# Two attentions on one core: products split and gating moved in the second, scaling and two peaks moved in the first

## The reference

```python
# first attention: 8 heads, two softmaxes per head, causal, blocks of 128 queries
s = einsum('bhqd,bshd->bhqs', qb, k) * scale
probs = softmax(where(mask, s, -inf))
a = probs(qb1, k1) - lam * probs(qb2, k2)
o = einsum('bhqs,bshe->bhqe', a, v)            # 128 values per head
o = rms(o, subln) * (1 - lambda_init) * silu(g)
x = x + o @ w_out

# second attention: 16 heads, stick breaking, causal, blocks of 128 queries
z = einsum('bhqd,bshd->bhqs', qb, k) * scale
log_1mb = where(mask, log_sigmoid(-z), 0)
suffix = cumsum(log_1mb, reverse) - log_1mb
a = where(mask, exp(log_sigmoid(z) + suffix), 0)
o = einsum('bhqs,bshe->bhqe', a, v)            # 64 values per head
x = x + (o * silu(g)) @ w_out
```

## Time and profile before

| | |
|---|---|
| median of 3 runs | 2500.83 us (2500.43 to 2504.84) |
| profiled execution, its own time | 2500.57 us |
| its span, first to last instruction | 2498.8 us |
| PE busy | 2352.5 us (94%) |
| DVE busy | 1519.7 us (61%) |
| ACT busy | 967.0 us (39%) |
| mean granted TensorE clock | 0.982 of full speed |

### The profile page before, as it was taken

How to read it: one execution, slowest core, us unless ns; L and a number is a source line. 1 busy time by engine, 2 the same in 40 slices (tenths; PEclk the granted TensorE clock), 3 DMA queues, 4 the chain that set the end, 5 groups by cost and what they waited for, 6 DMA issues and landing times.

```text
span 2498.8 us, 30214 instructions
## 1 busy us (share of the span) xinstructions
PE 2352.5 (94%) x12850; PEld 1248.1 (50%) x12850; DVE 1519.7 (61%) x1962; ACT 967.0 (39%) x1383; POOL 213.5 (9%) x258
## 2 busy tenths in 40 slices
PE   6999999999999999999999777899999997888899
PEld 3445444444444444444444455654444445766664
DVE  6898756644554355697631589955544307888861
ACT  5245334221212123333321476732223116777741
POOL 0001030000000002433202001022000000000000
PEclk9999999999999999999999899999999998999999
DMA  4010001211101110111110000110221100000021
GB/s 179 34 68 34 1 34 38 97 55 47 68 34 63 39 68 34 36 61 75 68 68 34 1 1 1 52 51 34 85 118 41 63 1 34 1 1 1 1 85 51
DMA packets 50328, 116.02 MB, mean 46 GB/s; under 512 B 2387, under 2 KB 7820, under 8 KB 49809
## 3 DMA queue, kind: packets, MB, share of 16 engines
q1 hardware_dynamic: 48456, 105.40, 11.9%
q10 hardware_dynamic: 1736, 8.68, 0.8%
HBM read 101.49 MB, written 12.58 MB: 46 GB/s over the span
## 4 chain that ended last, share of the span: by engine, by line
PE 79%; DVE 12%; ACT 6%; issue 2%; DMA 1%; ACTq 0%; POOL 0%; DVEq 0%
PE PS L72 76%; PE PS L75 4%; ACT RG L81 3%; DVE RG L107 2%; DVE R L101 2%; DVE R L93 2%; DVE mx L110 2%; DVE RG L101 1%; ACT OV L84 1%; DVE scl L110 1%; DMA RG<-in_a_w_in 1%; DVE RG L93 1%; ACT R L81 1%; DVE oss L110 1%; DVE mx L96 0%
## 5 line engine op out<-in xcount | busy, mean ns | idle before, releaser
L72 PE MATMUL PS<-R,RG 128*128 128x512 f16 (+1 forms) x5472 | 1167.6, 375 | 12.2 <-DVE RG L101 5.9
L72 PEld LDWEIGHTS PS<-R,RG 128*128 128x128 f16 (+1 forms) x5472 | 544.0, 104 | 632.2 <-issue 13.2
L72 PE MATMUL PS<-RG,R 128*128 128x512 f16 x2880 | 630.6, 379 | 3.5 <-DVE R L101 3.0
L72 PEld LDWEIGHTS PS<-RG,R 128*128 128x128 f16 x2880 | 281.7, 98 | 334.4 <-DVE R L101 3.5
L81 ACT ACTIVATE R<-PS,scl 128x512 f32<-128x512 f32 (+1 forms) x192 | 126.7, 686 | 711.6 <-PE PS L72 595.0
L101 DVE SCALAR_TENSOR_TENSOR R<-PS,scl,R 128x512 f32<-128x512 f32 (+1 forms) x208 | 148.6, 746 | 146.7 <-PE PS L72 121.6
L107 DVE TENSOR_TENSOR_SCAN RG<-RG 128x127 f32<-128x127 f32 (+7 forms) x128 | 168.6, 1345 | 109.9 <-ACT RG L81 109.6
L72 PE MATMUL PS<-R,OV 128*128 128x64 f32 (+2 forms) x1456 | 191.9, 284 | 33.3 <-DVE R L93 31.2
L101 DVE SCALAR_TENSOR_TENSOR RG<-RG,scl 128x4096 f16<-128x4096 f32 (+1 forms) x43 | 188.6, 4387 | 56.4 <-ACT RG L81 56.4
L72 PEld LDWEIGHTS PS<-R,OV 128*128 128x128 f32 x1456 | 179.1, 198 | 43.3 <-DVE R L93 37.7
L75 PE MATMUL PS<-ident,RG 128*128 128x128 f32 x864 | 149.4, 290 | 48.3 <-ACT OV L84 23.9
(11 more groups left out here) (123 smaller groups left out, 1541.0 us busy)
## 6 DMA issues: line engine op xcount, KB each, us to landing
RG<-in_w_ff SPq DMA_DIRECT2D x16, 2048.0 KB, 8.5
RG<-in_a_w_in SPq DMA_DIRECT2D x8, 2048.0 KB, 8.3
RG<-in_w_in SPq DMA_DIRECT2D x4, 2048.0 KB, 9.8
xspill<-R ACTq DMA_DIRECT2D x2, 4096.0 KB, 15.1
RG<-in_w_kv SPq DMA_DIRECT2D x4, 2048.0 KB, 8.0
RG<-in_b_w_in SPq DMA_DIRECT2D x4, 2048.0 KB, 7.9
R<-in_x SPq DMA_DIRECT2D x8, 512.0 KB, 9.2
RG<-in_w_out SPq DMA_DIRECT2D x2, 2048.0 KB, 7.8
```

The source lines that it names most:

```text
L72: return self.engine.matmul(*a, **k) if self.engine else Nothing()
```

## The change

In the second attention, PE's products of group u - 2 are cut into two halves by blocks of 128 keys: the first half stays behind the transposes of part 0, the second half goes behind the transposes of part 1. DVE's gating of group u - 3 moves from behind the scan of group u to ahead of it.

In the first attention, the scaling of the maxima leaves DVE: ACT scales them in place with a Copy activation just ahead of the Exp that uses them, and waits for its own result. It does this once for each group up to row 3, and once for each side from row 4 on. ACT's Square moves ahead of `exp(u, 1)`. The peak of GG's last tile and `o_peak` move from before the loop to the end of turn 3; `measure(31)` becomes four reductions of 1024 columns at the ends of turns 8 to 11 and a small one in turn 12.

```diff
@@ tensor, second attention
-                    if part == 0 and u >= 2:
+                    if u >= 2:
                         v = u - 2
                         i, hs = sb_groups[v]
-                        for x, h in enumerate(hs):
+                        blocks = [(x, h, j) for x, h in enumerate(hs) for j in range(i + 1)]
+                        mid = len(blocks) // 2
+                        for x, h, j in blocks[mid:] if part else blocks[:mid]:
                             g = h // 8
-                            if h % 8 == 0:
+                            if h % 8 == 0 and j == 0:
                                 banks.take_at(("pvb", i, g), 7)
                                 e.wait_ge(*banks.free(("pvb", i, g)))
                                 e.wait_ge(*sig("bank_act").at("v2", 1, NT - 1))
...
-                        mm.then_inc(*full.up("pvb", i, hs[-1]))
+                        if part:
+                            mm.then_inc(*full.up("pvb", i, hs[-1]))
@@ vector, before and in the first attention
+            def gate_peak(t):
+                e.wait_ge(*sig("gg_gain").at(t))
+                e.tensor_reduce(col(32 + t), GG[:, t, :], AX.X, ALU.max, apply_absolute_value=True).then_inc(*step.up())
...
-                e.wait_ge(*sig("gg_gain").at(t))
-                e.tensor_reduce(col(32 + t), GG[:, t, :], AX.X, ALU.max, apply_absolute_value=True).then_inc(*step.up())
-            e.wait_ge(*step.last())
-            e.tensor_reduce(col(123), col(32, 8), AX.X, ALU.max).then_inc(*sig("o_peak").up())
-            measure(31)
+                if t < NT - 1:
+                    gate_peak(t)
...
-                e.tensor_reduce(out, z, AX.X, ALU.max, negate=True).then_inc(*step.up())
-                e.wait_ge(*step.last())
-                e.tensor_scalar(m, m, ssc, None, ALU.mult).then_inc(*sig("top_a").up(u, sides[-1]))
+                e.tensor_reduce(out, z, AX.X, ALU.max, negate=True).then_inc(*sig("top_a").up(u, sides[-1]))
...
+                if u == 3:
+                    gate_peak(NT - 1)
+                    e.wait_ge(*step.last())
+                    e.tensor_reduce(col(123), col(32, 8), AX.X, ALU.max).then_inc(*sig("o_peak").up())
+                if 8 <= u < 12:
+                    j = u - 8
+                    e.wait_ge(*sig("raw").at(31))
+                    e.tensor_reduce(col(112 + j), w_raw(31)[:, 1024 * j:1024 * j + 1024], AX.X, ALU.max,
+                                    apply_absolute_value=True).then_inc(*step.up())
+                if u == 12:
+                    e.wait_ge(*step.last())
+                    e.tensor_reduce(w_col(31, 0), col(112, 4), AX.X, ALU.max).then_inc(*sig("w_peak").up(31))
@@ vector, second attention: the block "if u >= 3" with the gating, unchanged,
@@ stands ahead of the scan of group u instead of behind it and behind convert_low(40)
@@ scalar, first attention
+                if c == 0 or u >= da_first:
+                    m = da_scale(u, c)
+                    m = mx[:, m:m + len(hs) * (1 if u >= da_first else 2)]
+                    e.wait_ge(*sig("constants").at("ssc"))
+                    e.activation(m, m, ACT.Copy, scale=ssc).then_inc(*sig("top_scaled").up(u, c))
+                    e.wait_ge(*sig("top_scaled").at(u, c))
...
                 turned(u - 2, 1)
-                if u < N:
-                    exp(u, 1)
                 if 3 <= u < N + 3 and da_groups[u - 3][1][-1] % 4 == 3:
...
                     e.activation(sqb, bo, ACT.Square).then_inc(*sig("o_square").up(i, g))
+                if u < N:
+                    exp(u, 1)
                 turned(u - 1, 0)
```

More of the change, by code:

```diff
@@ L943, in tensor @@
                                 e.wait_ge(*sig("bank_act").at("v2", 1, NT - 1))
[L944 to L949, removed]
-                        mm.then_inc(*full.up("pvb", i, hs[-1]))
+                            at = width(i) * x + 128 * j
+                            e.wait_ge(*sig("turned_b").at(v, at // 512))
+                            mm = e.matmul(banks.ap(("pvb", i, g))[:, 64 * (h % 8):64 * (h % 8) + 64],
+                                          AT2[v % 2][:, at:at + 128], V2[:, j, 64 * h:64 * h + 64],
+                                          start=(j == 0), stop=(j == i))
+                        if part:
+                            mm.then_inc(*full.up("pvb", i, hs[-1]))
             gate_turn(0)
@@ L1600, in top @@
                 e.wait_ge(*full.at("za", u, sides[-1]))
-                e.tensor_reduce(out, z, AX.X, ALU.max, negate=True).then_inc(*step.up())
-                e.wait_ge(*step.last())
-                e.tensor_scalar(m, m, ssc, None, ALU.mult).then_inc(*sig("top_a").up(u, sides[-1]))
+                e.tensor_reduce(out, z, AX.X, ALU.max, negate=True).then_inc(*sig("top_a").up(u, sides[-1]))
             N = len(da_groups)
-            e.wait_ge(*sig("constants").at("ssc"))
             for u in range(N + 4):
@@ L1731, in vector @@
             for u in range(N + 3):
+                if u >= 3:
+                    i, hs = sb_groups[u - 3]
+                    if hs[-1] % 8 == 7:
+                        g = hs[-1] // 8
+                        gg = GG[:, i, cols512(g)]
+                        e.wait_ge(*full.at("pvb", i, hs[-1]))
+                        e.wait_ge(*sig("bank_act").at("g2", i, 1))
+                        e.tensor_tensor(gg, banks.ap(("pvb", i, g)), gg, ALU.mult).then_inc(
+                            *banks.empty([("pvb", i, g)], sig("g_gated"), i, g))
                 if u < N:
@@ L1741, in vector @@
                     convert_low(40)
[L1742 to L1750, removed]
                 if u < N:
```

## The result

| | before | after |
|---|---|---|
| median, 4 runs each on one chip | 2502.84 us (2500.43 to 2512.56) | 2472.55 us (2469.70 to 2473.07) |
| ratio | | 0.9869, 95% interval 0.9841 to 0.9898 |
| span of the profiled execution | 2498.8 us | 2470.4 us |
| DVE busy | 1519.7 us | 1501.4 us |
| ACT busy | 967.0 us | 984.3 us |

A forecast was written before the change was run, and what follows sets the result against it. PE's closed matmul chains fill most of the span; the change acts only in the two attentions, bound by waits among PE, DVE and ACT. Second attention -21.9 us, first -10.0, together -31.9 from 2500.57: 2469 us, range 2452 to 2488.

The forecast's parts named there:

- The gating ahead: Second attention, rows 4 to 7: DVE's gating before the scan frees bank 7 earlier, -15.6 us (-5 to -18).
- Turn 6 and the two gatings: Second attention: gating ahead of scan and conversion in turn 6, -5.0 us; other gatings in rows 2 and 3, -1.4.
- The split: Second attention: PE's products in two halves, losses in rows 2 and 4 against gains in 6 and 7, sum 0.1 us.
- My upper bound: Second attention, cutting the products: at worst 0.3 us more in each of 40 groups of rows 2, 4, 5, +10 us.
- The plain pair of row 4: Second attention: two groups with their scores take 5.5 us instead of 5.02, PE waiting 0.5 us before part 1.
- Slower: PE's clock: Second attention: two short idles a group in rows 2, 4, 5 keep TensorE at 1.2 GHz; 2524 us, chance 0.07.
- Peaks: First attention: first maximum starts 5.9 us earlier, but the moved reductions cost it again later; sum 0 (-4 to +2).
- Scaling in rows 0 to 3: First attention: DVE gives up 22 small scalings to ACT, -1.0 us.
- Square in rows 1 to 3: First attention: Square before the second Exp shortens two DVE waits by 1.0 us and five by 0.6, -5.0 us.
- The ring: First attention from row 4: cycle of maximum, scaling, Exp, next scores, next maximum; grows from 4.22 to 4.32 us a turn.
- the gating turn: First attention from row 4: a turn with gating falls from 5.84 to 5.05 us, -0.8 each in eight rounds.
- The other signs: Expected in the profile: shorter waits for gating, sigmoids and Square, higher granted clock, first maximum near 1392.6, small Copy 0.30 us.

The follow-up runs named there:

- peak last: Changed kernel with the second attention's eight row peaks reduced behind the loop instead of in it; 2465.45 us, ratio 0.9864.
- late halves: Row peaks as two 512-column reductions, two turns after their gatings: changed kernel unsplit 2456.27 us; changed kernel with products cut behind the fourth block 2453.30 us.

## Why the prediction was right, and where it was not

**The gating ahead: right.** Forecast -15.6 us in rows 4 to 7, measured -14.2 alone, and -19.4 in the second profile of the same code. One step on the way was not as I had it. I left 2.8 us of waiting for bank 7 and nothing for the join that now stands behind the waiting gating and the scan. PE waits 0.7 us for the bank and 7.6 us for the join (with the gating alone 6.8 us in six waits, none for the bank), so its waits for DVE hardly fall. What falls are DVE's waits for the sigmoids, 31.4 to 15.3 us.

**Rows 1 to 3 of the second attention: right, a little more than forecast.** Turn 6 and the two gatings were to give -6.4 us, the split +2.0 in row 2. That is -4.4; the change has -6.3 in rows 1 to 3 (87.0 to 80.7), the unsplit one -9.3.

**The split: this step failed.** I made its sum, 0.1 us, on the kernel before, at full clock, and there it holds in the mean (-2.7 us in rows 4 to 7, forecast -1.9). In the changed kernel it costs 12.4 us from row 2 on, after less unsplit: row 2 +2.3, row 3 0, row 4 +7.7, row 5 +1.9, row 6 -0.3, row 7 +0.9. Some of this is the luck of a profile: against the other one of the same unsplit code it is 5.1 us in rows 4 to 7 instead of 10.2, with row 4 +6.1. My upper bound was +10 (0.3 us in 40 groups is 12). The plain pair of row 4 was right, 5.44 us (2172.26 to 2177.70) for a forecast of 5.5, and the idle time before part 1 is 0.28 us instead of 0.5. What I left out is their coming together with a longer wait. Row 4 in six versions:

| row 4, us | whole peak | peak last | late halves |
|---|---|---|---|
| split in half (4 matmuls first) | 50.65 | 44.57 | |
| split behind four (8 matmuls first) | 44.50 | | 42.57 |
| unsplit (10 matmuls) | 42.97, 44.52 | | 42.43 |

The two values of the unsplit row are those of the change without the split and of the gating-ahead version. The row with the split in half and the whole peak has 50.67 in a second profile. Against the unsplit row with late halves (42.43) the whole peak alone costs 0.5 or 2.1 us and the short first half alone 2.1 us. Both together cost 8.2. That is the rival "Slower: PE's clock", which I priced with every pair of rows 2 and 4 at the lower level, +55 us. It came true for some 13 us of row 4 (2155.5 to 2168), and in the change nowhere else for so long.

One rule had been weighed against the traces. The Trainium skill, TensorE: Matmul & The Clock Gate, "A second HAM failure mode: psum-queue depth-cycling", has short idles between groups let the clock swing. The runs agree only in part: in the first 26 us of row 4 the clock granted was 1.00 with the 0.28 us idles and no long wait, and 0.77 with both.

**The peak reduction: not in my sum.** I counted 18.4 us of DVE's waits to the turns behind the gatings and left 0.35 us of waiting for each. In every second gating turn a further 1.2 us stands on DVE, ahead of the next scan. The conversion in turn 6 I had looked for, this one not. Taken in late halves the peaks bring the unsplit kernel from 217.7 to 213.5 us in rows 4 to 7. The medians differ by more, from -37.4 to -48.5 us against before. 4.1 of these 11 us lie in the medians of the kernel before itself (2500.66 and 2504.78); the versions' own medians are 7.0 us apart, and some 3 us of that I can't place in the rows.

**The first attention: right in direction, too small.** Peaks 0: measured 0. Scaling in rows 0 to 3: -1.0 forecast, +1.0 measured. Square in rows 1 to 3: -5.0, measured -5.8. Rows 4 to 7: -4.0 forecast, -10.2 measured (157.3 to 147.1). The ring was right (4.30 for 4.32, with 298 ns for 0.30 us). The term that was mis-sized is the gating turn: in row 6, 35.55 us for six plain turns of 4.30 leave 4.88 us for each of two, where I had 5.05; before it is 5.92 by the same sum, where I had 5.84. (The terms that I wrote down for it add up to 5.87.) That is 1.04 us a turn instead of 0.8, and it explains 1.9 of the 6.2 us. Another 2.7 us are not the change's. In the profile of the kernel before row 4 takes 37.55 us and row 7 48.26; in the profiles of the split alone and the gating alone, where the first attention is the same code, it is 36.5 and 46.6. At the end of row 7 the same sixteen products behind the same wait show the difference, first before, then the split alone:

```profile
1621.63 0.66 PE L75 MATMUL PS<-ident,RG 128*128 128x128 f32 x4 [2.51 <-DVE RG L101]
1622.12 3.42 PE L72 MATMUL PS<-R,RG 128*128 128x128 f32 x16
```

```profile
1620.37 0.66 PE L75 MATMUL PS<-ident,RG 128*128 128x128 f32 x4 [2.51 <-DVE RG L101]
1620.87 1.95 PE L72 MATMUL PS<-R,RG 128*128 128x128 f32 x16
```

So the edits of the first attention are worth about 7.4 us in rows 4 to 7, and the last 1.6 us lie in the ends of rows 4 and 7, which I did not price.

**The other signs.** DVE's waits for the sigmoids 15.3 us (forecast 14), for Square 4.6 (4), first maximum at 1394.70, which is 1392.6 if the 2.1 us later start is taken off: right. "Waits of PE for L93 fall to about 3": by the bank alone 0.7, with the join 8.3, so wrong in what it stands for. "Granted clock up from 0.95": wrong, 0.94.

## What to carry to other kernels

When an instruction is put ahead of others on a busy engine, look for what comes only once in many turns in the same turn, a reduction or a conversion: the turn that has both sets the longest wait, and such work can be cut and moved to a turn that has neither. Price an edit in the kernel that it will stand in: the split was neutral by itself and cost 7 us in the medians against before, 5 to 10 in rows 4 to 7, once the gating was ahead, and the scaling on ACT gained nothing until Square had left the way. And where a cut is made by halves, try the place of the cut: behind the fourth block instead of the middle made rows 4 to 7 11 us shorter (227.9 to 216.8), 9 of them in rows 4 and 5. Where a row holds a stretch of low clock, look for a second profile of the same code before a difference is put down to an edit.

## What the runs showed of the hardware

The length of a wait doesn't say which clock TensorE runs at behind it, not even in the same code. Behind 1.43 us with ten products in one piece it stayed at the 2.4 GHz level in one profile (0.99 us for twelve scores) and fell to 1.2 GHz in another (1.78 us). Behind the 2.51 us at the end of row 7 of the first attention it fell in four of six profiles (before, Square ahead alone, peaks alone, change without the scaling) and not in two (split alone, gating ahead alone); with the scaling on ACT and Square ahead that wait is 1.82 us, and it fell in none of seven.

How long the lower level lasts did depend on the code. In row 4 of the second attention it was over with the next group where the products came in one piece, lasted some 13 us in both profiles with the products in pieces of four and six behind a wait of 1.18 us, and with pieces of eight and two it was back within two groups behind 1.62 us. Why it lasts is not shown by these runs. They show that the long stretch in row 4 came only with both the long wait and the short first piece.

At the start of the second attention the clock differs between profiled executions, also where an edit changes nothing there: with the scaling alone row 1 takes 27.6 us against 20.4 before. Windows that lie in row 1, of the gating-ahead version (row 1 is 2072.65 to 2100.29 there) and of the change (2060.52 to 2079.36):

```profile
2080.00:2110.00 30.00, 29.92 (x157) 24.32 (x151) 21.39 (x23) 17.10 (x20) 0.76 (x1) 0.50 0.08 24
```

```profile
2060.00:2080.00 20.00, 17.28 (x161) 13.76 (x156) 18.49 (x26) 16.31 (x19) 0.65 (x1) 0.93 0.00 1
```

At 0.50 row 1 takes 27.3 to 27.6 us, otherwise 18 to 20. It happened in three of the twelve experiments' profiles (split alone, gating ahead alone, scaling alone). The eight runs of the gating-ahead version lie from 2474.39 to 2490.73 us; its profile is the longest, and its mean granted clock is the lowest, 0.979, against 0.984 to 0.988 in the six runs up to 2477.60 us. A profile alone would have ranked the versions wrongly: row lengths outside such a stretch and the medians together did not.
